# Modulation vectors on one Trainium2 core: four chunks collected in one PSUM bank by zero-spaced stationary columns, and read out by one copy and four transposes

## The chip, the cores and the metric

The kernel runs on one core of one Trainium2 chip. The time is the device time of one execution in microseconds (us), the median of three runs.

## The reference

Two blocks of a network follow each other on 256 tokens of width 2048, in float32. The first block has two attention layers (even and odd), each `x + (y @ w_out)` with an input projection `rms_norm(x) @ w_in`. The second block has a gated linear recurrence and a differential attention, and both are modulated by a condition:

```python
sc = jax.nn.silu(c)
scc = jax.nn.silu(c_ctx)
for i in range(DEPTH):
    shift, scale, gate = jnp.split(sc @ mod_w[i] + mod_b[i], 3, axis=-1)
    cshift, cscale, cgate = jnp.split(scc @ mod_w[i] + mod_b[i], 3, axis=-1)
    h_lat = rms_norm_2(x, norm_g[i]) * (1.0 + scale[:, None]) + shift[:, None]
    h_ctx = rms_norm_2(ctx, norm_g[i]) * (1.0 + cscale) + cshift
```

`mod_w` is 2 x 2048 x 6144. What is changed is the way the products `sc @ mod_w[i]` and `scc @ mod_w[i]` are collected and turned into columns: two rows (the two conditions) times 21 chunks of 512 outputs. (Three more chunks of the second layer are made elsewhere, in the second block, and stay as they are.)

## The kernel before, in words

**Units and the ring.** All weights come through a ring of 8 slots (`ring`, `raw(U)`), in units of 128 x 1024 float32 (512 KB): two k-tiles of 128 rows by 512 columns. The list `RING` sets the order of all units of the program; SyncE's queue loads unit U as soon as TensorE has used unit U - 8. A unit of a projection is split by ScalarE into a high part (`ring_hi`, line 1427) and by VectorE into a low part (`ring_lo`, line 1954), and TensorE multiplies high by high, low by high and high by low: 12 matmuls of 512 columns a unit in `multiply` (line 782).

**The modulation.** 168 of the first block's units are modulation units, 8 to a chunk of 512 outputs, laid in pairs between the projection units (`with_mod`). They are not split: `fill_mod` (line 855) multiplies them as plain float32. The stationary operand holds the conditions' columns, the moving one the weights. K-tile k goes to the 32 PSUM partitions that start at 32 * (k % 4), so that each of the four groups of 32 partitions of bank 3 holds a quarter of the sum over k. The matmul's stationary operand is 32 columns wide, of which two matter (the two conditions). All this happens in the first block's stretch of the program, between its heads' work.

**Reading a chunk out.** When the 8 units of chunk m are through, VectorE copies the bank to SBUF (`mod_rows`, line 2042). Later, ahead of the last projection unit that stands before chunk m + 1, TensorE runs `sum_mod` (line 866): four float32 matmuls with 128 columns of the copied rows as the stationary operand and the two columns of `row_sums` as the moving one (`SEL` holds ones at partitions 0, 32, 64, 96 for condition 0, and at the next ones for condition 1). They add the four quarters and turn the rows into columns at once, and write them into the same bank 3. VectorE then adds the bias and stores to `mod_t` (`mod_columns`, line 2050). The first matmul of chunk m + 1 waits for that (`mod_ready`). In the trace each plain float32 matmul stands as two records, with two LDWEIGHTS records; a transpose stands as one.

**VectorE's order.** `follow(units)` walks the same list: at the unit in `ROWS_BY` it copies the rows, at the unit in `SUMS_BY` it makes the columns, after the splits that are due there. A wait in it holds back everything behind it on VectorE.

Of the kernel before, what the change touches and what calls it, by code (L numbers as in the profile page):

```python
# [24 lines left out]
ALU = mybir.AluOpType  # L25
AX = mybir.AxisListType.X

P = 128
SEQ = 256
D = 2048  # L30
KT = D // P
TT = SEQ // P
# [38 lines left out]
CHUNK = 512  # L71
# [151 lines left out]
def chunk_units(stage, chunks, per=8):  # L223
# [63 lines left out]
POS = {unit: at for at, unit in enumerate(RING)}  # L287
# [80 lines left out]

ROWS_BY = {next(s for s in SPLIT_UNITS if s > POS["mod", 8 * m + 7]): m for m in range(N_MOD)}
SUMS_BY = {max(s for s in SPLIT_UNITS if s < POS["mod", 8 * m + 8]): m for m in range(N_MOD - 1)}  # L370
SUMS_BY[POS[OD_TURNS[-1].gaps[1][1]]] = N_MOD - 1
assert len(ROWS_BY) == len(SUMS_BY) == N_MOD and all(r <= s for r, s in zip(sorted(ROWS_BY), sorted(SUMS_BY)))

# [48 lines left out]
RES0 = {"ev_out": 0, "od_out": 4, "lru_out": 8, "att_out": 13}  # L422
MODS_BEFORE_MLA = sum(POS["mod", 8 * m + 7] < POS["ukv", 0] for m in range(N_MOD))
FEATURES_LAT, FEATURES_OD, FEATURES_CTX = 24, 27, 35
# [5 lines left out]
def build(nc, t, consts, out):  # L430
    ctx = ExitStack()
    with ctx:
        def sb(name, shape, dtype=F32, owner=ctx):
            return owner.enter_context(nc.sbuf_tensor(name, shape, dtype))
# [35 lines left out]

        def raw(U, n=UNIT):

            return RA[:, U % SLOTS, 0:n]
# [108 lines left out]
        s_hi, s_lo, s_lop, s_wused = map(sem, ("weights_hi", "weights_lo_by_vector", "weights_lo_by_gpsimd", "weight_units_used"))  # L582
        s_vt, s_vec, s_cond, s_cs = map(sem, ("vectors_transposed", "vectors_ready", "cond_hi", "cond_ready"))
        s_sq, s_sqc, s_ms, s_rt, s_rs = map(sem, ("squares_summed", "chunk_squares_summed", "mean_square", "root_taken", "rstd_ready"))
# [178 lines left out]
        def _(pe):  # L763
# [82 lines left out]
            def fill_mod(u):  # L846

                m, j = divmod(u, 8)
                U = POS["mod", u]
# [9 lines left out]
            def sum_mod(m, bank=MB):  # L859

                pe.wait_ge(s_mods, m + 1)
                if m:
                    pe.wait_ge(s_modd, m)
                rows = MODS_EV if m < MODS_OF_EVEN else MODS_OD
# [29 lines left out]
            def head_turn(turn):  # L894
# [76 lines left out]
                if turn is MLA_TURNS[1]:  # L971
                    pe.wait_ge(s_ge, evicted("ukv", 3))
                    pe.wait_ge(s_mods, MODS_BEFORE_MLA)
                    y_transposes_of("ev", 4)
                    y_transposes_of("ev", 5)
# [109 lines left out]
            def od_out(u):  # L1085
                c, j = divmod(u, 9)
                hold = None
                if u == 0:
                    hold = {1: (s_ge, evicted("od_c", 0))}
                elif j == 0:  # L1090
                    hold = {m: (s_re, RES0["od_out"] + c - 1) for m in range(TT)} if c >= 2 else {0: (s_ye, len(YT)), 1: (s_modd, N_MOD)}
                multiply(POS["od_out", u], 2 * j, 2, 18, CHUNK, [(m, 2 * (c % 2) + m) for m in range(TT)], xt, hold=hold)
# [223 lines left out]
            def gate_sums(i):  # L1316

                pe.wait_ge(s_gm, i * 16 + 16)
                for k in range(4):
                    mm = pe.matmul(PS[:, 7, 2 * P + k:2 * P + k + 1], GACC[:, k * P:(k + 1) * P], SEL[:, 2:3], start=True, stop=True)  # L1320
                mm.then_inc(s_gsum, 1)
# [620 lines left out]
        def _(dve):  # L1942
            steps = [0]

            def link(ins):

                steps[0] += 1
                ins.then_inc(s_dve, 1)
                dve.wait_ge(s_dve, steps[0])
# [89 lines left out]

            def mod_rows(m):  # L2040
                dve.wait_ge(s_wused, POS["mod", 8 * m + 7] + 1)
                dve.tensor_copy(MODS_EV if m < MODS_OF_EVEN else MODS_OD, PS[:, 3, :]).then_inc(s_mods, 1)

            def mod_columns(m, bank=3):

                dve.wait_ge(s_modt, m + 1)
                layer, c = MOD_CHUNK[m]
# [121 lines left out]
            dve.wait_ge(s_const, 16)  # L2169
            dve.tensor_reduce(SEL[:, 0:2], ident.rearrange("p (g w) -> p w g", g=4)[:, 0:2, :], AX, ALU.add)  # L2170
            dve.memset(SEL[:, 2:3], 1.0)
            for u in range(5):
# [116 lines left out]

            dve.wait_ge(s_modd, N_MOD)  # L2290
            for l in range(2):
# [528 lines left out]
```

## Time and profile before

| | |
|---|---|
| median of three runs (2495.31 to 2495.77) | 2495.64 us |
| span of the profiled execution | 2493.0 us |
| TensorE matmul busy | 2472.9 us, 99% of the span |
| VectorE busy | 1478.2 us, 59% |
| ScalarE busy | 1179.3 us, 47% |
| TensorE's granted clock | 1.000 of full speed, the whole span |

For the profiled execution only the span is given, from its first to its last instruction; the median of the runs is 2.6 us above it. PE is TensorE's matmuls and PEld its weight loads, DVE is VectorE, ACT ScalarE, SPq SyncE's queue. Matmuls are pipelined: a record lasts longer than the step from one start to the next, so costs on TensorE are read from starts, not from durations.

### The profile page before, as it was taken

To read this page: it belongs to the slowest core of one execution; us is meant where nothing else is said; L and a number is where in the kernel's file an instruction comes from. 1 tells how busy PE (TensorE), PEld (TensorE's weight loads), DVE (VectorE), ACT (ScalarE), POOL (GpSimd) and SP (SyncE) were. 2 spreads that over 40 slices of the span, in tenths; PEclk is the share of its full clock that TensorE was granted. 3 is DMA by queue.
4 is the path that set the end of the run, shared out by engine and by line. 5 is a ranking of instruction groups with operands and counts; after the bars stand their busy time and mean duration, and the time that the engine had idled before them with its cause. 6 is when DMAs were issued, how large, how long until landed. Compare 5 with 4: busy or idle time off the path is not lost.

```text
span 2493.0 us, 31492 instructions
## 1 busy us (share of the span) xinstructions
PE 2472.9 (99%) x11984; PEld 1941.0 (78%) x11984; DVE 1478.2 (59%) x1951; ACT 1179.3 (47%) x1742; POOL 265.2 (11%) x140
## 2 busy tenths in 40 slices
PE   8999999999999999999999999999999999999999
PEld 7887777777777777788777777788887887877877
DVE  6644445554545554566767677734746476665775
ACT  6644444653444444456565555624525334243463
POOL 0000000000000000002555555100300000000000
PEclk9999999999999999999999999999999999999999
DMA  7567777637787777764333332324434344344334
GB/s 278 172 216 260 249 258 247 234 103 242 231 279 243 253 261 246 251 225 149 102 95 95 89 96 88 118 93 136 136 108 152 127 127 151 111 151 128 129 106 152
DMA packets 278403, 429.43 MB, mean 172 GB/s; under 512 B 14582, under 2 KB 93196, under 8 KB 277644
## 3 DMA queue, kind: packets, MB, share of 16 engines
q1 hardware_dynamic: 277532, 422.54, 52.1%
q10 hardware_dynamic: 752, 5.26, 0.5%
q8 instruction: 80, 1.31, 0.2%
q14 instruction: 39, 0.32, 0.0%
HBM read 425.64 MB, written 2.10 MB: 172 GB/s over the span
## 4 chain that ended last, share of the span: by engine, by line
PE 96%; ACT 1%; DVE 1%; DMA 1%; issue 0%; POOL 0%; SPq 0%; DVEq 0%; ACTq 0%
PE ps L782 67%; PE ps L1174 13%; PE ps L855 3%; PE ps L1157 2%; PE ps L964 1%; PE ps L1285 1%; PE ps L937 1%; PE ps L1303 1%; PE ps L833 1%; PE ps L1129 1%; PE ps L866 1%; PE ps L949 1%; DMA ring<-in_att_w_in 0%; PE ps L1294 0%; PE ps L1192 0%
## 5 line engine op out<-in xcount | busy, mean ns | idle before, releaser
L1427 ACT CAST ring_hi<-ring 128x1024 fp32r<-128x1024 f32 (+2 forms) x598 | 619.9, 1039 | 953.9 <-PE ps L782 533.2
L1954 DVE TENSOR_TENSOR ring_lo<-ring,ring_hi 128x1024 fp32r<-128x1024 f32 (+2 forms) x520 | 626.8, 1210 | 633.6 <-ACT ring_hi L1427 631.3
L782 PE MATMUL ps<-ring_hi,act_hi 128*128 128x512 f32 (+2 forms) x1272 | 512.8, 403 | 0.7 <-ACT proj L1506 0.6
L782 PE MATMUL ps<-ring_hi,act_lo 128*128 128x512 f32 (+2 forms) x1272 | 491.7, 387 | 0.0
L782 PE MATMUL ps<-ring_lo,act_hi 128*128 128x512 f32 (+2 forms) x1272 | 490.3, 385 | 0.0
L782 PE MATMUL ps<-ring_hi,features_hi 128*128 128x512 f32 x1152 | 457.6, 397 | 1.1 <-ACT second_block L1744 0.9
L782 PE MATMUL ps<-ring_hi,features_lo 128*128 128x512 f32 x1152 | 449.2, 390 | 0.0
L782 PE MATMUL ps<-ring_lo,features_hi 128*128 128x512 f32 x1152 | 448.7, 389 | 0.0
L782 PEld LDWEIGHTS ps<-ring_hi,act_hi 128*128 128x128 f32 x1272 | 239.4, 188 | 102.1 <-issue 41.4
L782 PEld LDWEIGHTS ps<-ring_hi,act_lo 128*128 128x128 f32 x1272 | 239.2, 188 | 50.8
L782 PEld LDWEIGHTS ps<-ring_lo,act_hi 128*128 128x128 f32 x1272 | 240.0, 189 | 41.9
L782 PEld LDWEIGHTS ps<-ring_hi,features_hi 128*128 128x128 f32 x1152 | 216.4, 188 | 63.8 <-issue 20.3
L782 PEld LDWEIGHTS ps<-ring_hi,features_lo 128*128 128x128 f32 x1152 | 216.2, 188 | 45.9
L782 PEld LDWEIGHTS ps<-ring_lo,features_hi 128*128 128x128 f32 x1152 | 216.6, 188 | 42.3
L2748 POOL TENSOR_TENSOR ring_lo<-ring,ring_hi 128x1024 fp32r<-128x1024 f32 x78 | 210.0, 2700 | 338.7 <-ACT ring_hi L1427 338.6
L1174 PE MATMUL ps<-features_hi,ring_hi 128*128 128x512 f32 x480 | 192.8, 402 | 0.0
L1174 PE MATMUL ps<-features_lo,ring_hi 128*128 128x512 f32 x480 | 186.8, 389 | 0.0
L1174 PE MATMUL ps<-features_hi,ring_lo 128*128 128x512 f32 x480 | 186.8, 389 | 0.0
L1174 PEld LDWEIGHTS ps<-features_lo,ring_hi 128*128 128x128 f32 x480 | 90.1, 188 | 21.8 <-issue 3.6
L1174 PEld LDWEIGHTS ps<-features_hi,ring_hi 128*128 128x128 f32 x480 | 90.1, 188 | 21.8 <-issue 3.6
L1174 PEld LDWEIGHTS ps<-features_hi,ring_lo 128*128 128x128 f32 x480 | 90.1, 188 | 18.7
L855 PE MATMUL ps<-ring,cond_t 128*32 128x512 f32 x672 | 89.5, 605 | 0.0
(277 smaller groups left out, 2453.4 us busy)
## 6 DMA issues: line engine op xcount, KB each, us to landing
ring<-in_mod_w SPq DMA_DIRECT2D x192, 512.0 KB, 5.2
ring<-in_att_w_in SPq DMA_DIRECT2D x128, 512.0 KB, 3.7
ring<-in_ev_w_in SPq DMA_DIRECT2D x104, 512.0 KB, 4.8
ring<-in_od_w_in SPq DMA_DIRECT2D x96, 512.0 KB, 4.6
ring<-in_lru_w_in SPq DMA_DIRECT2D x64, 512.0 KB, 4.0
ring<-in_ev_w_out SPq DMA_DIRECT2D x40, 512.0 KB, 4.5
ring<-in_lru_w_out SPq DMA_DIRECT2D x40, 512.0 KB, 3.7
ring<-in_od_w_out SPq DMA_DIRECT2D x36, 512.0 KB, 4.9
```

What stands on the lines that cost most here:

```text
L782: mm = pe.matmul(PS[:, bank, 0:n], a, w[:, k - k0, :], start=(k == k_first and j == 0), stop=(k == k_last and j == 2))
L833: mm = pe.transpose(PS[:, 4 + q % 4, col:col + P], rows(tt, 2 * j + k), ident)
L855: mm = pe.matmul(PS[g:g + 32, MB, :], CS[:, 2 * k:2 * k + 32], raw(U)[:, k % 2 * CHUNK:(k % 2 + 1) * CHUNK], start=(k < 4), stop=(k >= KT ...
L866: mm = pe.matmul(PS[:, bank, 2 * j:2 * j + 2], rows[:, j * P:(j + 1) * P], SEL[:, 0:2], start=True, stop=True)
L937: mm = pe.matmul(to, qt[:, tt * P:(tt + 1) * P], kt_[:, 0:n], start=True, stop=h is not MLA)
L949: mm = pe.transpose(PS[:, 4 + a, h.p_at(kt, tt):h.p_at(kt, tt) + P], S[:, a, s:s + P], ident)
L964: mm = pe.matmul(PS[:, 6 + a, tt * P:tt * P + w], PT[:, a, h.p_at(kt, tt):h.p_at(kt, tt) + P], rows, start=(kt == 0), stop=(kt == kts[-1]))
L1157: mm = pe.matmul(PS[:, 4 + j, :], GW[:, b, j, :], XC[:, b, :, :].rearrange("p c s -> p (c s)"), start=True, stop=True)
L1174: mm = pe.matmul(PS[:, part * 2 + b, :], W[:, w], x[:, kk, :], start=(kk == 0 and j == 0), stop=(kk == KT - 1 and j == 2))
L1427: act.copy(high(U, n), raw(U, n)).then_inc(s_hi, 1)
L1954: dve.tensor_tensor(out=low(U, n), in0=raw(U, n), in1=high(U, n).bitcast(F32), op=ALU.subtract).then_inc(s_lo, 1)
L2748: pool.tensor_tensor(out=low(U), in0=raw(U), in1=high(U).bitcast(F32), op=ALU.subtract).then_inc(s_lop, 1)
```

## The change

Four chunks now form a round (the last round has one chunk: 21 chunks make 6 rounds). The conditions' columns are stored with zeros between them in `CZ`, part of the tile `scalars`: k-tile k's two columns stand at 8 * (k + 1) - 2. A window of 8 columns that starts 2 * slot earlier holds them at places 2 * slot and 2 * slot + 1, with zeros in the other six. So chunk `slot` of a round adds its two rows at its own partitions of each group and adds zeros to the others', and the stationary operand is 8 columns wide where it was 32. The bank is copied, transposed (four transposes of 128 x 128 in place of four matmuls with two columns) and reduced once a round. The sum over the four groups is now made by VectorE, one `tensor_reduce` for each condition, and the bias is added to 16 x 2 columns at once. The order of the chunks over the ring's modulation units is changed so that a round lies in one layer; which ring positions are modulation units is not.

```diff
-MODS_OF_EVEN = 12
-MOD_CHUNK = [(0, m) for m in range(10)] + [(1, 11)] + [(1, m) for m in range(8)] + [(0, 10), (0, 11)]
+MOD_CHUNK = [(0, m) for m in range(12)] + [(1, m) for m in range(8)] + [(1, 11)]
+MOD_SLOTS = 4
+MOD_COLS = 2 * MOD_SLOTS
+N_ROUND = -(-N_MOD // MOD_SLOTS)
+ROUNDS_OF_EVEN = 3
+def round_chunks(r):
+
+    return range(r * MOD_SLOTS, min((r + 1) * MOD_SLOTS, N_MOD))
+def round_end(r):
+
+    return 8 * round_chunks(r)[-1] + 7
...
+ROWS_BY = {next(s for s in SPLIT_UNITS if s > POS["mod", round_end(r)]): r for r in range(N_ROUND)}
+SUMS_BY = {max(s for s in SPLIT_UNITS if s < POS["mod", round_end(r) + 1]): r for r in range(N_ROUND - 1)}
...
-        SEL = sb("row_sums", [P, 3])
+        SEL = sb("row_sums", [P, 1])
+        CZ = SC[:, 0:(KT + 1) * MOD_COLS - 2]
...
-                if j == 0 and m:
-                    pe.wait_ge(s_modd, m)
+                if slot == 0 and j == 0 and r:
+                    pe.wait_ge(s_modd, r)
                 pe.wait_ge(s_w[U % SLOTS], landed(U))
                 for k in range(2 * j, 2 * j + 2):
-                    g = 32 * (k % 4)
-                    mm = pe.matmul(PS[g:g + 32, MB, :], CS[:, 2 * k:2 * k + 32], raw(U)[:, k % 2 * CHUNK:(k % 2 + 1) * CHUNK],
-                                   start=(k < 4), stop=(k >= KT - 4))
+                    g, first = 32 * (k % 4), (k + 1) * MOD_COLS - 2 - 2 * slot
+                    mm = pe.matmul(PS[g:g + MOD_COLS, MB, :], CZ[:, first:first + MOD_COLS], raw(U)[:, k % 2 * CHUNK:(k % 2 + 1) * CHUNK],
+                                   start=(slot == 0 and k < 4), stop=(m == round_chunks(r)[-1] and k >= KT - 4))
...
+                rows = MODS_EV if r < ROUNDS_OF_EVEN else MODS_OD
                 for j in range(4):
-                    mm = pe.matmul(PS[:, bank, 2 * j:2 * j + 2], rows[:, j * P:(j + 1) * P], SEL[:, 0:2], start=True, stop=True)
+                    mm = pe.transpose(PS[:, bank, j * P:(j + 1) * P], rows[:, j * P:(j + 1) * P], ident)
                 mm.then_inc(s_modt, 1)
...
-            pe.wait_ge(s_cs, 1)
+            pe.wait_ge(s_cz, 1)
...
+            def mod_columns(r, bank=3):
+
+                dve.wait_ge(s_modt, r + 1)
+                n = len(round_chunks(r))
+                layer, c = MOD_CHUNK[round_chunks(r)[0]]
                 first = VEC_AT["mod_b_2"] + 48 * layer + 4 * c
-                sums = PS[:, bank, 0:8].rearrange("p (k w) -> p k w", w=2)
-                dve.tensor_tensor(out=MODT[:, layer, 4 * c:4 * c + 4, :], in0=sums, in1=GT[:, first:first + 4].unsqueeze(2).to_broadcast([P, 4, 2]),
+                cols = MODT[:, layer, 4 * c:4 * c + 4 * n, :]
+                parts = PS[:, bank, :].rearrange("p (b g q) -> p b g q", b=4, g=4)
+                for w in range(2):
+                    ins = dve.tensor_reduce(cols[:, :, w].rearrange("p (s b) -> p s b", b=4),
+                                            parts[:, :, :, w:2 * n:2].rearrange("p b g s -> p s b g"), AX, ALU.add)
+                link(ins)
+                dve.tensor_tensor(out=cols, in0=cols, in1=GT[:, first:first + 4 * n].unsqueeze(2).to_broadcast([P, 4 * n, 2]),
                                   op=ALU.add).then_inc(s_modd, 1)
...
             dve.sem_inc(s_ltab, 1)
+            link(dve.memset(CZ, 0.0))
+            dve.wait_ge(s_cs, 1)
+            dve.tensor_copy(CZ[:, MOD_COLS - 2:].rearrange("p (k q) -> p k q", q=MOD_COLS)[:, :, 0:2],
+                            CS[:, 0:2 * KT].rearrange("p (k v) -> p k v", v=2)).then_inc(s_cz, 1)
```

On TensorE, behind the first chunk (`proj` is where the copied rows lie, `ring_hi`, `ring_lo` and `act_hi`, `act_lo` are the split weights and activations of a projection), before:

```order
L782 MATMUL ps<-ring_hi,act_lo 128x512
L866 MATMUL ps<-row_sums,proj 128x2 [waits mod_rows_ready]
L866 MATMUL ps<-row_sums,proj 128x2 x3
L782 MATMUL ps<-ring_hi,act_hi 128x512 [waits weights_lo_by_vector]
L782 MATMUL ps<-ring_lo,act_hi 128x512
```

The same place now:

```order
L796 MATMUL ps<-ring_hi,act_hi 128x512
L796 MATMUL ps<-ring_lo,act_hi 128x512
L796 MATMUL ps<-ring_hi,act_lo 128x512
L796 MATMUL ps<-ring_hi,act_hi 128x512 [waits weights_lo_by_vector]
L796 MATMUL ps<-ring_lo,act_hi 128x512
```

The two rows of `row_sums` are gone there, and the projection goes on without a break; this happens behind 15 of the 21 chunks.

On TensorE, behind the fourth chunk, which ends the first round, before (the last row is the next modulation unit's first matmul):

```order
L866 MATMUL ps<-row_sums,proj 128x2 [waits mod_ready,mod_rows_ready]
L866 MATMUL ps<-row_sums,proj 128x2 x3
L782 MATMUL ps<-ring_hi,act_hi 128x512 [waits weights_lo_by_vector]
...
L782 MATMUL ps<-ring_hi,act_lo 128x512
L855 MATMUL ps<-ring,cond_t 32x512 [waits weights_landed2,mod_ready]
L855 MATMUL ps<-ring,cond_t 32x512
```

The same place now:

```order
L879 MATMUL ps<-consts,proj 128x128 [waits mod_rows_ready]
L879 MATMUL ps<-consts,proj 128x128 x3
L796 MATMUL ps<-ring_hi,act_hi 128x512 [waits weights_lo_by_vector]
...
L796 MATMUL ps<-ring_hi,act_lo 128x512
L870 MATMUL ps<-ring,scalars 8x512 [waits weights_landed2,mod_ready]
L870 MATMUL ps<-ring,scalars 8x512
```

Four transposes stand where the four matmuls stood, one projection unit (12 matmuls) ahead of the next modulation unit, as before, and that unit still waits for `mod_ready`.

On VectorE at the same end of a round, before:

```order
L1954 TENSOR_TENSOR ring_lo<-ring,ring_hi 128x1024 [waits weights_hi]
L2042 COPY proj<-ps 128x512 [waits weight_units_used]
L1954 TENSOR_TENSOR ring_lo<-ring,ring_hi 128x1024 [waits weights_hi] x2
L2050 TENSOR_TENSOR mod_t<-ps,vectors_t 128x8 [waits mod_summed]
L1954 TENSOR_TENSOR ring_lo<-ring,ring_hi 128x1024 [waits weights_hi]
```

And now:

```order
L1967 TENSOR_TENSOR ring_lo<-ring,ring_hi 128x1024 [waits weights_hi]
L2055 COPY proj<-ps 128x512 [waits weight_units_used]
L1967 TENSOR_TENSOR ring_lo<-ring,ring_hi 128x1024 [waits weights_hi] x2
L2066 TENSOR_REDUCE mod_t<-ps 128x16 [waits mod_summed]
L2066 TENSOR_REDUCE mod_t<-ps 128x16
L2069 TENSOR_TENSOR mod_t<-mod_t,vectors_t 128x32 [waits vector_step]
L1967 TENSOR_TENSOR ring_lo<-ring,ring_hi 128x1024 [waits weights_hi]
```

Three linked instructions stand where one stood, still behind the two splits.

## Rows read from the trace of the kernel before

**Rows 1.** The page: span, and busy time of each engine
```profile
span 2493.0 us, 31492 instructions
PE 2472.9 (99%) x11984; PEld 1941.0 (78%) x11984; DVE 1478.2 (59%) x1951; ACT 1179.3 (47%) x1742; POOL 265.2 (11%) x140
```

**Rows 2.** Windows: length, busy of PE, PEld, DVE, ACT, POOL, PEclk, DMA share, GB/s
```profile
170.00:1060.00 890.00, 887.79 (x4622) 662.08 (x4621) 456.46 (x741) 397.48 (x611) 1.99 (x4) 1.00 0.72 240
```

**Rows 3.** The page: the chain that ended last, by engine
```profile
PE 96%; ACT 1%; DVE 1%; DMA 1%; issue 0%; POOL 0%; SPq 0%; DVEq 0%; ACTq 0%
```

**Rows 4.** Line 855, the modulation units' matmuls: duration ns min/median/max, first and last start
```profile
L855 PEld LDWEIGHTS ps<-ring,cond_t x672: 105/108/110, 175.2 to 1047.8; 128*32 128x32 f32 x168
L855 PE MATMUL ps<-ring,cond_t x672: 592/604/618, 175.2 to 1048.2; 128*32 128x512 f32 x168
```

**Rows 5.** Line 866, the sums of the first twelve chunks
```profile
L866 PEld LDWEIGHTS ps<-row_sums,proj x96: 187/192/192, 200.7 to 755.5; 128*128 128x128 f32 x96
L866 PE MATMUL ps<-row_sums,proj x96: 165/251/251, 200.9 to 755.6; 128*128 128x2 f32 x96
```

**Rows 6.** Timeline of PE around one pair of modulation units: start us, us
```profile
174.88 0.39 PE L782 MATMUL ps<-ring_hi,act_lo 128*128 128x512 f32 x1
175.20 1.07 PE L855 MATMUL ps<-ring,cond_t 128*32 128x512 f32 x8
176.20 0.50 PE L782 MATMUL ps<-ring_hi,act_hi 128*128 128x512 f32 x1
176.53 0.39 PE L782 MATMUL ps<-ring_lo,act_hi 128*128 128x512 f32 x1
176.76 0.39 PE L782 MATMUL ps<-ring_hi,act_lo 128*128 128x512 f32 x1
```

**Rows 7.** Timeline of PE around one sum
```profile
200.70 0.39 PE L782 MATMUL ps<-ring_hi,act_lo 128*128 128x512 f32 x1
200.93 0.95 PE L866 MATMUL ps<-row_sums,proj 128*128 128x2 f32 x8
201.74 0.49 PE L782 MATMUL ps<-ring_hi,act_hi 128*128 128x512 f32 x1
202.06 0.40 PE L782 MATMUL ps<-ring_lo,act_hi 128*128 128x512 f32 x1
```

**Rows 8.** Timeline of PE around four transposes
```profile
65.84 0.39 PE L782 MATMUL ps<-ring_hi,mem_lo 128*128 128x512 f32 x1
66.07 0.60 PE L833 MATMUL ps<-consts,x_res 128*128 128x128 f32 x4
...
66.73 0.39 PE L782 MATMUL ps<-ring_lo,mem_hi 128*128 128x512 f32 x1
```

**Rows 9.** Timeline at the end of the fourth chunk's sum (the window cuts off L855)
```profile
320.77 0.16 DVE L2050 TENSOR_TENSOR mod_t<-ps,vectors_t 128x8 f32<-128x8 f32 x1
321.33 0.64 PE L855 MATMUL ps<-ring,cond_t 128*32 128x512 f32 x4
```

**Rows 10.** Timeline at the end of the twelfth chunk's sum
```profile
758.33 0.39 PE L782 MATMUL ps<-ring_hi,act_lo 128*128 128x512 f32 x1
758.45 0.16 DVE L2050 TENSOR_TENSOR mod_t<-ps,vectors_t 128x8 f32<-128x8 f32 x1
758.66 0.64 PE L855 MATMUL ps<-ring,cond_t 128*32 128x512 f32 x4
```

**Rows 11.** Timeline at the end of the twentieth chunk's sum
```profile
1033.83 0.17 DVE L2050 TENSOR_TENSOR mod_t<-ps,vectors_t 128x8 f32<-128x8 f32 x1 [3.30 <-PE ps L866]
1035.26 0.64 PE L855 MATMUL ps<-ring,cond_t 128*32 128x512 f32 x4
```

**Rows 12.** Groups of DVE: busy us, mean ns of one, idle before
```profile
L1984 DVE TENSOR_REDUCE stats<-scalars 128x2 f32<-128x8 f32 x2 | 0.3, 162 | 3.1 <-ACT second_block L1460 3.1
L2195 DVE TENSOR_REDUCE scalars<-arena 128x2 f32<-128x128 f32 x1 | 0.3, 286 | 0.0
```

**Rows 13.** Waits of ACT between 170 and 1060 us, for the weights to land
```profile
ACT ring_hi L1427 <- DMA ring<-in_od_w_in: 145.0, 69, 6.7
```

More of the change, by code:

```diff
@@ L367 @@
 LAST_OF = {multiplied(*chunk) - 1: chunk for chunk in EVICTED}
[L369 to L372, printed above, removed]
+ROWS_BY = {next(s for s in SPLIT_UNITS if s > POS["mod", round_end(r)]): r for r in range(N_ROUND)}
+SUMS_BY = {max(s for s in SPLIT_UNITS if s < POS["mod", round_end(r) + 1]): r for r in range(N_ROUND - 1)}
+SUMS_BY[POS[OD_TURNS[-1].gaps[1][1]]] = N_ROUND - 1
+assert len(ROWS_BY) == len(SUMS_BY) == N_ROUND and all(r <= s for r, s in zip(sorted(ROWS_BY), sorted(SUMS_BY)))
 def evicted(stage, c):
@@ L422 @@
 RES0 = {"ev_out": 0, "od_out": 4, "lru_out": 8, "att_out": 13}
-MODS_BEFORE_MLA = sum(POS["mod", 8 * m + 7] < POS["ukv", 0] for m in range(N_MOD))
+ROUNDS_BEFORE_MLA = sum(POS["mod", round_end(r)] < POS["ukv", 0] for r in range(N_ROUND))
 FEATURES_LAT, FEATURES_OD, FEATURES_CTX = 24, 27, 35
@@ L848, in fill_mod, with sum_mod @@
                 m, j = divmod(u, 8)
+                r, slot = divmod(m, MOD_SLOTS)
                 U = POS["mod", u]
-                if j == 0 and m:
-                    pe.wait_ge(s_modd, m)
+                if slot == 0 and j == 0 and r:
+                    pe.wait_ge(s_modd, r)
                 pe.wait_ge(s_w[U % SLOTS], landed(U))
                 for k in range(2 * j, 2 * j + 2):
-                    g = 32 * (k % 4)
-                    mm = pe.matmul(PS[g:g + 32, MB, :], CS[:, 2 * k:2 * k + 32], raw(U)[:, k % 2 * CHUNK:(k % 2 + 1) * CHUNK],
-                                   start=(k < 4), stop=(k >= KT - 4))
+                    g, first = 32 * (k % 4), (k + 1) * MOD_COLS - 2 - 2 * slot
+                    mm = pe.matmul(PS[g:g + MOD_COLS, MB, :], CZ[:, first:first + MOD_COLS], raw(U)[:, k % 2 * CHUNK:(k % 2 + 1) * CHUNK],
+                                   start=(slot == 0 and k < 4), stop=(m == round_chunks(r)[-1] and k >= KT - 4))
                 mm.then_inc(s_wused, 1)
[L859 to L864, printed above, removed]
+            def sum_mod(r, bank=MB):
+                pe.wait_ge(s_mods, r + 1)
+                rows = MODS_EV if r < ROUNDS_OF_EVEN else MODS_OD
                 for j in range(4):
-                    mm = pe.matmul(PS[:, bank, 2 * j:2 * j + 2], rows[:, j * P:(j + 1) * P], SEL[:, 0:2], start=True, stop=True)
+                    mm = pe.transpose(PS[:, bank, j * P:(j + 1) * P], rows[:, j * P:(j + 1) * P], ident)
                 mm.then_inc(s_modt, 1)
@@ L972, in head_turn @@
                     pe.wait_ge(s_ge, evicted("ukv", 3))
-                    pe.wait_ge(s_mods, MODS_BEFORE_MLA)
+                    pe.wait_ge(s_mods, ROUNDS_BEFORE_MLA)
                     y_transposes_of("ev", 4)
@@ L1090, in od_out @@
                 elif j == 0:
-                    hold = {m: (s_re, RES0["od_out"] + c - 1) for m in range(TT)} if c >= 2 else {0: (s_ye, len(YT)), 1: (s_modd, N_MOD)}
+                    hold = {m: (s_re, RES0["od_out"] + c - 1) for m in range(TT)} if c >= 2 else {0: (s_ye, len(YT)), 1: (s_modd, N_ROUND)}
                 multiply(POS["od_out", u], 2 * j, 2, 18, CHUNK, [(m, 2 * (c % 2) + m) for m in range(TT)], xt, hold=hold)
@@ L1319, in gate_sums @@
                 for k in range(4):
-                    mm = pe.matmul(PS[:, 7, 2 * P + k:2 * P + k + 1], GACC[:, k * P:(k + 1) * P], SEL[:, 2:3], start=True, stop=True)
+                    mm = pe.matmul(PS[:, 7, 2 * P + k:2 * P + k + 1], GACC[:, k * P:(k + 1) * P], SEL[:, 0:1], start=True, stop=True)
                 mm.then_inc(s_gsum, 1)
@@ L2038, in residual_add, with mod_rows @@
                 ins.then_inc(s_re, 1)
[L2040 to L2047, printed above, removed]
-                first = VEC_AT["mod_b_2"] + 48 * layer + 4 * c
-                sums = PS[:, bank, 0:8].rearrange("p (k w) -> p k w", w=2)
-                dve.tensor_tensor(out=MODT[:, layer, 4 * c:4 * c + 4, :], in0=sums, in1=GT[:, first:first + 4].unsqueeze(2).to_broadcast([P, 4, 2]),
+            def mod_rows(r):
+                dve.wait_ge(s_wused, POS["mod", round_end(r)] + 1)
+                dve.tensor_copy(MODS_EV if r < ROUNDS_OF_EVEN else MODS_OD, PS[:, 3, :]).then_inc(s_mods, 1)
+            def mod_columns(r, bank=3):
+                dve.wait_ge(s_modt, r + 1)
+                n = len(round_chunks(r))
+                layer, c = MOD_CHUNK[round_chunks(r)[0]]
+                first = VEC_AT["mod_b_2"] + 48 * layer + 4 * c
+                cols = MODT[:, layer, 4 * c:4 * c + 4 * n, :]
[5 more added lines that the diff above has]
+                dve.tensor_tensor(out=cols, in0=cols, in1=GT[:, first:first + 4 * n].unsqueeze(2).to_broadcast([P, 4 * n, 2]),
                                   op=ALU.add).then_inc(s_modd, 1)
@@ L2169, in _ @@
             dve.wait_ge(s_const, 16)
-            dve.tensor_reduce(SEL[:, 0:2], ident.rearrange("p (g w) -> p w g", g=4)[:, 0:2, :], AX, ALU.add)
-            dve.memset(SEL[:, 2:3], 1.0)
+            dve.memset(SEL[:], 1.0)
             for u in range(5):
@@ L2288, in _ @@
             follow([("od_out", u) for u in range(3, 6)])
-            dve.wait_ge(s_modd, N_MOD)
+            dve.wait_ge(s_modd, N_ROUND)
             for l in range(2):
```

2 lines of the change are left out of this document (1 added, 1 removed).

## The prediction

> **What bounds the kernel now.** I read the page first. TensorE's matmuls are busy for 2472.9 of 2493.0 us and the granted clock is full throughout [rows 1, 2], and the chain that ended last runs through TensorE for 96% [rows 3]. In the stretch that holds all modulation work, 170 to 1060 us, TensorE is busy for 887.79 of 890 us, while VectorE and ScalarE are at about half and the DMA engines at 0.72 [rows 2]. So the reader is to see that whatever is taken off TensorE's queue there comes off the time, as long as the others can follow, and that work taken off VectorE is worth nothing by itself.
>
> Next I read the two lines that the change touches. Line 855 has 672 records of which each lasts 604 ns, in 84 pairs of units with eight records each [rows 4]. Line 866 has 96 records in the first twelve of the 21 sums, eight in each [rows 5]. Records overlap, so I took the cost of each group from the starts around it. The yardstick is the step of product matmuls, 176.53 to 176.76, 0.23 us [rows 6]. From the last product matmul ahead of a group to the second one behind it would be two such steps, 0.46 us, if the group were not there; I take the second one, since the first behind a group starts its successor late as well.
>
> - A pair of modulation units: 174.88 to 176.53 is 1.65 us, so it costs 1.19 us [rows 6], and 84 of them 100 us.
> - A sum: 200.70 to 202.06 is 1.36 us, so it costs 0.90 us [rows 7], and 21 of them 18.9 us.
> - Four transposes in the same surroundings: 65.84 to 66.73 is 0.89 us, so they cost 0.43 us [rows 8].
>
> The sum is dear for what it does because it loads 128 columns of stationary data eight times (192 ns a record, rows 5) to move two columns through; the transposes have four records.
>
> **The change, part by part.**
>
> *The sums go.* 21 x 0.90 = 18.9 us less on TensorE. Nothing hides this time today: the products stand in the same queue.
>
> *The transposes come.* Six rounds of four: 6 x 0.43 = 2.6 us more. The Trainium skill speaks for a higher price here ("TensorE: Matmul & The Clock Gate", Part 4, PE-mode transpose): it gives about 275 ns for a transpose within a kernel; an estimate with that figure is 24 x 0.275 = 6.6 us, and the sum would be 4 us worse. The rows have the same shape and type in the same kind of stream, four in 0.43 us, and I go by them.
>
> *The stationary operand shrinks from 32 to 8 columns.* The number of matmuls, the moving columns (512) and the groups of PSUM partitions they go to stay. What can change is the load of the stationary operand. No row has 8 columns. The nearest rows are 108 ns at 32 columns [rows 4] and 192 ns at 128 columns [rows 5], both float32 matmuls in two records: 84 ns for 96 columns, so 24 columns fewer are 21 ns a load. How many loads lie on the path? At least none: 84 x 0 = 0. At most all eight of a pair: 84 x 8 x 0.021 = 14.1 us. Eight records of 604 ns pass in 1.00 us (175.20 to 176.20, rows 6), so four run side by side and their loads too; the first load of a pair must lie open, since nothing runs in front of it. I take one: 84 x 0.021 = 1.8 us less.
>
> *VectorE's copies and adds.* 15 copies and 15 adds go and 12 reductions come. VectorE is about half idle in this stretch [rows 2], so that is zero. The cover is its idle time. If it were gone, TensorE would wait for low parts of weights.
>
> *The end of a round.* Here the change can make a new wait. TensorE runs one projection unit behind the transposes and then needs `mod_ready`. Before, VectorE's part was one add of 0.16 us. Now it is two reductions, a link and an add over 32 elements. The reductions read 64 elements; the nearest rows are 162 ns for 8 elements and 286 ns for 128 [rows 12], so about 0.22 us. Two of them and a last step like today's add, less what two neighbours on VectorE overlap, make about 0.60 us, 0.44 us more than today. Moreover TensorE arrives there earlier by 0.90 - 0.43 = 0.47 us, while VectorE at this place hangs behind splits that wait for weights to land or for the heads' softmax, not for the sum. So `mod_ready` comes up to 0.91 us later as seen from TensorE. Against that stand the margins of today, from the end of the add to the start of the next modulation pair: 321.33 - 320.93 = 0.40 us at the first round's end [rows 9], 758.66 - 758.61 = 0.05 us at the third's [rows 10], 1035.26 - 1034.00 = 1.26 us at the fifth's [rows 11]. At 0.05 us there is no stall yet, since the pair starts 0.33 us after the last product matmul [rows 10], as elsewhere (0.32, rows 6), but nothing to spare either; so 0.35 us can be spared at the first and 1.21 us at the fifth. That gives a wait of 0.91 - 0.35 = 0.56 us at the first, 0.91 us at the third and none at the fifth. The second's and the fourth's margins are larger than the fifth's. Sum 1.5 us more. The lower end is 0.5 us (VectorE moves along with TensorE), the upper end 2.5 us (reductions as dear as 0.4 us each). Behind the waiting matmul stand all later products, so such a wait is paid in full. VectorE itself only waits for the transposes, which come sooner than the sums did.
>
> *The last round* has one chunk and is read out where it was read out before. The wait for `mod_ready` behind it stands at the second output chunk of the odd layer, nine units later, and costs nothing.
>
> *The zeros.* One memset and one copy on VectorE, at about 107 us, before TensorE's first modulation pair at 175.2 us [rows 4]: some 0.4 us in VectorE's idle time, so zero. If it came late, TensorE's first pair would wait, once.
>
> The sum, against the median: 2495.64 - 18.9 + 2.6 - 1.8 + 1.5 = 2479.0 us. The durations come from one execution with a span of 2493.0 us, 2.6 us below the median; that rest lies outside the first and last instruction and I leave it as it is. In its terms the span should be 2476.4 us.
>
> **The rivals.**
>
> *All loads of a pair lie on the path.* The gain is 12.3 us more: 2466.7 us. Against it stands that eight records pass in 1.00 us. The Trainium skill ("TensorE: Matmul & The Clock Gate", LDWEIGHTS) counts a load by its columns, columns / 1.2 in ns; by that rule 24 columns are worth 20 ns, and the trace's 21 ns agrees. Chance 0.05.
>
> *The weights cannot follow.* ScalarE waits for landings for 145.0 us on the odd layer's weights alone, 69 times [rows 13]; the splits come as late as the data. If TensorE gets ahead in this stretch, it may find the low parts missing and give part of the gain back. Against it: the DMA engines are at 0.72 and TensorE loses only 2.2 us of 890 today [rows 2], and the demand rises by 16/890, less than 2%. Given back in half, the time is 2487 us (chance 0.07); given back in full, 2495.5 us (chance 0.05).
>
> *The narrow matmuls do not run side by side: slower.* If a stationary operand of 8 columns were not treated as one group of the array, as that of 32 is, a pair would take eight steps one after another. A start-to-start step of a record cannot be less than its 0.23 us (a product matmul of the same 512 columns), so 1.8 us in place of 1.00; with two passes a record, 0.46 us, it is 3.7 us. 84 pairs make +67 to +227 us: 2546 to 2706 us. It turns the sign from 16.6 / 84 = 0.2 us a pair on. For it speaks only that no row has so narrow an operand; against it, that the output still starts at partitions 0, 32, 64 and 96. Chance 0.03.
>
> **How the numbers follow.** The forecast (2479 us, own range 2475 to 2483) has a chance of 0.80, and the rivals 0.05, 0.07, 0.05 and 0.03. The range is 2472 to 2486 us: it takes the forecast with its bounds and half of each neighbouring case, and leaves out less than 2 in 10. 0.2% is 5 us, about what a measurement can tell from no change here. Faster by more than that are the forecast, the open loads and the half given back: 0.92, of which I take 0.01 off for a mishap in between. Within 0.2%: 0.05. Slower: 0.04.
>
> **What would show it.** In the profile after, line 866's eight records a chunk are gone, and 24 records of transposes stand for them; the starts around a pair of modulation units are 1.63 us apart where they were 1.65; PE's busy time falls by some 18 us and its idle time rises by about 1.5 us, at the ends of the first and third round, with the reductions' add named as what ended it. VectorE's reductions should last about 0.22 us. The granted clock stays 1.00. The prediction is wrong if TensorE shows new waits for `ring_lo` in this stretch, if the eight records of a pair take more than 1.0 us, or if the transposes of a round take more than 0.43 us.

## The result, and the profile after

The changed kernel takes 2478.64 us (median of 4 runs, 2477.48 to 2479.91) against 2495.47 us of the kernel before on the same chip (4 runs, 2494.67 to 2495.77). The ratio is 0.9933, with a 95% interval of 0.9921 to 0.9945: 16.8 us or 0.67% faster, where 16.6 us were forecast. The profiled execution took 2478.72 us, of which its span is 2476.9.

The page of the changed kernel, its head, answers to [rows 1]:

```profile
span 2476.9 us, 31153 instructions
## 1 busy us (share of the span) xinstructions
PE 2455.2 (99%) x11840; PEld 1921.5 (78%) x11840; DVE 1469.1 (59%) x1934; ACT 1179.1 (48%) x1742; POOL 265.2 (11%) x140
```

TensorE has 144 matmul records fewer (168 of the sums gone, 24 transposes new) and 17.7 us less busy time; it is still the engine that sets the time. VectorE lost 9.1 us, which by itself buys nothing.

The modulation matmuls (line 870, which was 855) of the changed kernel, duration ns min/median/max, against [rows 4]:

```profile
L870 PEld LDWEIGHTS ps<-ring,scalars x672: 85/88/90, 175.2 to 1030.4; 128*8 128x8 f32 x168
L870 PE MATMUL ps<-ring,scalars x672: 592/594/597, 175.2 to 1030.9; 128*8 128x512 f32 x168
```

Around the first pair, the timeline of TensorE against [rows 6] (start us, us):

```profile
174.88 0.39 PE L796 MATMUL ps<-ring_hi,act_lo 128*128 128x512 f32 x1
175.20 1.04 PE L870 MATMUL ps<-ring,scalars 128*8 128x512 f32 x8
176.17 0.50 PE L796 MATMUL ps<-ring_hi,act_hi 128*128 128x512 f32 x1
176.51 0.39 PE L796 MATMUL ps<-ring_lo,act_hi 128*128 128x512 f32 x1
```

A load is 20 ns shorter (88 for 108), and so is the whole pair: 174.88 to 176.51 is 1.63 us where it was 1.65. Eight loads became shorter, and the pair gained the time of one. The four groups of PSUM partitions still work side by side: eight records of 0.59 us each pass in 0.97 us (175.20 to 176.17).

Around the first round's transposes, against [rows 7] and [rows 8]:

```profile
314.15 0.39 PE L796 MATMUL ps<-ring_hi,act_lo 128*128 128x512 f32 x1
314.38 0.60 PE L879 MATMUL ps<-consts,proj 128*128 128x128 f32 x4
314.74 0.47 PE L796 MATMUL ps<-ring_hi,act_hi 128*128 128x512 f32 x1
315.05 0.39 PE L796 MATMUL ps<-ring_lo,act_hi 128*128 128x512 f32 x1
```

From 314.15 to 315.05 is 0.90 us, less two steps of 0.23: 0.44 us for a group of four, as in [rows 8].

What TensorE waited for between 170 and 1060 us in the changed kernel (us in total, times, longest):

```profile
PE ps L870 <- DVE mod_t L2069: 0.8, 1, 0.8
PE ps L922 <- ACT proj L1519: 0.8, 1, 0.8
PE ps L796 <- ACT proj L1519: 0.6, 1, 0.6
PE ps L922 <- DVE arena L2265: 0.5, 1, 0.5
PE ps L977 <- DVE arena L2150: 0.2, 1, 0.2
```

Two of the five are new. The second, third and fourth stand in the kernel before too, with the same 0.8, 0.6 and 0.5 us. The first is new; it lies at the third round's end, against [rows 10]:

```profile
748.11 0.21 DVE L2066 TENSOR_REDUCE mod_t<-ps 128x16 f32<-128x64 f32 x1
...
748.36 0.19 DVE L2069 TENSOR_TENSOR mod_t<-mod_t,vectors_t 128x32 f32<-128x32 f32 x1
748.60 0.12 PEld L870 LDWEIGHTS ps<-ring,scalars 128*8 128x8 f32 x8 [1.25 <-DVE mod_t L2069]
748.60 1.04 PE L870 MATMUL ps<-ring,scalars 128*8 128x512 f32 x8 [0.83 <-DVE mod_t L2069]
```

The last is new as well. It lies behind the last round's read-out, where VectorE's reductions and add stand ahead of two copies to `arena` that TensorE's line 977 needs:

```profile
1040.80 0.25 DVE L2066 TENSOR_REDUCE mod_t<-ps 128x4 f32<-128x16 f32 x2
1041.08 0.17 DVE L2069 TENSOR_TENSOR mod_t<-mod_t,vectors_t 128x8 f32<-128x8 f32 x1
1041.17 1.28 DVE L2150 COPY arena<-ps 128x512 f32<-128x512 f32 x2
1041.10 0.60 PE L893 MATMUL ps<-consts,proj 128*128 128x128 f32 x4
1041.90 1.83 PE L977 MATMUL ps<-mem_kv,arena 128*128 128x128 f32 x14 [0.21 <-DVE arena L2150]
```

The same place before:

```profile
1058.16 0.16 DVE L2050 TENSOR_TENSOR mod_t<-ps,vectors_t 128x8 f32<-128x8 f32 x1
1058.23 1.28 DVE L2131 COPY arena<-ps 128x512 f32<-128x512 f32 x2
1058.91 0.60 PE L880 MATMUL ps<-consts,proj 128*128 128x128 f32 x4
1059.35 1.39 PE L964 MATMUL ps<-mem_kv,arena 128*128 128x128 f32 x11
```

From the four transposes (line 893, before 880) to the matmul that needs the copies it is 0.80 us, where it was 0.44. With the 0.1 us by which the matmul behind it starts late as well, the place costs 0.5 us.

**A yardstick for all runs.** All kernels here run the same other instructions on TensorE. So I took the starts of the same two of them, a product matmul at about 135 us and a transpose at about 1065 us, on either side of all modulation work, and compared the stretch between. It leaves out what differs from execution to execution at the start and behind. Each stretch is that of one execution, and its landings of weights differ: two executions of the changed kernel agree within 0.06 us, but one place, told below, moved by up to 0.5 us.

| kernel | stretch, us | against before | median, us | median of the kernel before, beside it |
|---|---|---|---|---|
| before | 930.20 | | 2495.47 | |
| changed | 912.84 | -17.36 | 2478.64 | 2495.47 |
| changed, again | 912.90 | -17.30 | 2478.11 | 2494.95 |
| narrow only | 928.52 | -1.68 | 2492.88 | 2494.95 |
| rounds of one chunk | 920.14 | -10.06 | 2487.90 | 2494.95 |
| third round earlier | 912.24 | -17.96 | 2477.08 | 2494.95 |
| sums twice | 948.78 | +18.58 | 2520.98 | 2495.39 |
| half more sums | 941.17 | +10.97 | 2504.26 | 2495.01 |
| transposes twice | 914.63 | -15.57 | 2479.94 | 2495.39 |
| fours | 913.17 | -17.03 | 2479.16 | 2495.39 |
| fours and earlier | 911.38 | -18.82 | 2479.25 | 2495.39 |
| late fours | 910.42 | -19.78 | 2475.57 | 2495.01 |

### The profile page after: what moved, and what is told of

Read it like the earlier page. It is cut to its first block, busy times and chain, and to the rows that moved or that the text cites. A ratio compares the mean times of both kernels' runs of the same rounds, so it can differ in the third digit from the quotient of the medians.

```text
span 2476.9 us, 31153 instructions
## 1 busy us (share of the span) xinstructions
PE 2455.2 (99%) x11840; PEld 1921.5 (78%) x11840; DVE 1469.1 (59%) x1934; ACT 1179.1 (48%) x1742; POOL 265.2 (11%) x140
## 4 chain that ended last, share of the span: by engine, by line
PE 96%; DVE 1%; ACT 1%; DMA 1%; issue 1%; POOL 0%; SPq 0%; DVEq 0%; ACTq 0%
PE ps L796 67%; PE ps L1187 13%; PE ps L870 3%; PE ps L1170 2%; PE ps L977 1%; PE ps L1298 1%; PE ps L950 1%; PE ps L1316 1%; PE ps L847 1%; PE ps L1142 1%; PE ps L962 1%; DMA ring<-in_att_w_in 1%; PE ps L1307 0%; PE ps L1205 0%; ACT ring_hi L1440 0%
## 5 line engine op out<-in xcount | busy, mean ns | idle before, releaser
L1187 PEld LDWEIGHTS ps<-features_hi,ring_lo 128*128 128x128 f32 x480 | 90.1, 188 | 18.7
L870 PE MATMUL ps<-ring,scalars 128*8 128x512 f32 x672 | 87.8, 594 | 0.8 <-DVE mod_t L2069 0.8
```

What stands on the lines that cost most here:

```text
L870: mm = pe.matmul(PS[g:g + MOD_COLS, MB, :], CZ[:, first:first + MOD_COLS], raw(U)[:, k % 2 * CHUNK:(k % 2 + 1) * CHUNK], start=(slot == 0 ...
L1187: mm = pe.matmul(PS[:, part * 2 + b, :], W[:, w], x[:, kk, :], start=(kk == 0 and j == 0), stop=(kk == KT - 1 and j == 2))
```

## The experiments

The theory is that of the prediction: the time is TensorE's own, 0.9 us a sum and 0.43 us a group of transposes, one open load a pair, and a wait where a round's end has no time to spare. The rivals: all loads of a pair lie on the path; or what counts is how seldom VectorE copies and waits; or the stretch behind, not the change, accounts for part of it.

**The changed kernel again**, unedited.

> The changed kernel once more, unedited, to tell what belongs to it from what belongs to one execution. Theory: the first block again ends some 17.3 us earlier than in the kernel before, and the 1.3 us that the profiled execution gave back between 1900 and 2250 us, far behind the change, come out at another size, between 0 and 3 us; median 2478.6 within 1.5 us. Rival, that the give-back is caused by the shifted work: it has the same size and stands at the same places again.

Median 2478.11 us, ratio 0.9933 (0.9919 to 0.9946). The stretch is the same within 0.06 us. Behind it, the two changed executions differ: 1424.01 us from the transpose at 1048 us to the last matmul in the first, 1422.97 in this one, 1422.65 in the kernel before. So 1.0 of the 1.3 us that the first profile lost there belong to that execution, and the change's own gain in the stretch is 17.3 us. Not all of it reaches the time: the medians are 16.8 us apart in both measurements, so about 0.5 us are given back outside the stretch. The other kernels with transposes lose between 0.4 and 2.5 us behind it in their profiles, narrow only and half more sums 0.1 us; why is not shown.

**Narrow only.**

```diff
-                    mm = pe.matmul(PS[g:g + 32, MB, :], CS[:, 2 * k:2 * k + 32], raw(U)[:, k % 2 * CHUNK:(k % 2 + 1) * CHUNK],
+                    mm = pe.matmul(PS[g:g + 8, MB, :], CS[:, 2 * k:2 * k + 8], raw(U)[:, k % 2 * CHUNK:(k % 2 + 1) * CHUNK],
```

> The kernel before, with the stationary operand cut from 32 to 8 columns and nothing else; the 6 columns beside the two conditions are those of the next k-tiles, and the sums leave their rows out. Theory of one open load a pair: 84 x 0.02 = 1.7 us less, about 2493.8 us. Rival of all eight loads on the path: 14 us less, about 2481.5 us. Rival that the width costs nothing: 2495.5 us.

Median 2492.88 us, ratio 0.9992 (0.9983 to 1.0001). The medians are 2.1 us apart, which the interval does not tell from nothing; the stretch, 1.68 us shorter, does: it is 84 x 0.020. All eight loads on the path would have been 14 us. The part that is left, 17.36 - 1.68 = 15.7 us, comes from the read-out.

**Rounds of one chunk.**

```diff
-MOD_SLOTS = 4
+MOD_SLOTS = 1
-ROUNDS_OF_EVEN = 3
+ROUNDS_OF_EVEN = 12
```

> The changed kernel with rounds of one chunk: 21 copies, 21 groups of four transposes, 42 reductions, and 2 columns of stationary data. It changes the kind of read-out without making it rarer. Theory, by TensorE's time alone: 15 more groups of transposes at 0.43 us are 6.5 us more than the changed kernel, 6 columns fewer are 0.4 us less, and the ends of chunks that have no time to spare (the third, fourth and sixth round's places and others like them, 0.05 to 0.7 us of margin today) wait for the longer chain, 1 to 4 us: 2486 to 2489 us. Rival, that what counts is how seldom VectorE copies and waits: the gain is gone with the rarity, 2495 us.

Median 2487.90 us, ratio 0.9971 (0.9961 to 0.9982). VectorE copies as often as before, waits for TensorE as often and has more to do, and the kernel is 7 us faster: rarity is not what counts for VectorE. TensorE's terms give the stretch: 21 x (0.44 - 0.90) = -9.7, and the pair, with 2 columns, is 26 ns shorter than with 32 (gap of 1288 ns for 1314), -2.2. The waits of TensorE show what was given back:

```profile
PE ps L870 <- DVE mod_t L2069: 1.6, 3, 0.7
```

That view counts only the time in which no matmul ran. By the gaps around the five pairs that start late it is 2.1 us, and the wait behind the last read-out, the same as in the changed kernel, is another 0.5: -9.7 - 2.2 + 2.1 + 0.5 = -9.3, where -10.06 was measured. The other 0.8 us lie in many steps of under 0.1 us each, and I can't name their cause. The median gained only 7.05 us: 3.0 us are lost outside the stretch, 2.5 of them behind it in the profile (last section). So the median fell into the expected 2486 to 2489 us with the help of a loss that the expectation didn't have. Of the 16.3 us that the read-out gains with rounds of four, 9.7 thus come from the kind of operation, and 6.6 from having six groups of transposes on TensorE and not 21. The kind gains because four transposes are four records and four float32 matmuls are eight: the starts of both are 0.11 us apart, whether 128 columns move or two.

**Sums twice, and half more.** The kernel before with `for j in (0, 1, 2, 3) * 2`, and in a second kernel `for j in (0, 1, 0, 1, 2, 3)`, around the sum's matmuls.

```diff
-                for j in range(4):
+                for j in (0, 1, 2, 3) * 2:
                     mm = pe.matmul(PS[:, bank, 2 * j:2 * j + 2], rows[:, j * P:(j + 1) * P], SEL[:, 0:2], start=True, stop=True)
```

> The kernel before with each chunk's four sum matmuls run twice in a row, the second time over the same result. Theory, that a sum's price is TensorE's own time: eight more records of 0.1 us each and no new turn of the stream, so 21 x 0.86 = 18 us more, about 2513 us. Rival, that the sums were cheap and the gain came from VectorE's copies and waits: nearly nothing more, 2495 to 2498 us. Some of it may be a little higher, where the add already came just in time (0.05 us of margin at four places): up to 3 us more.

> The kernel before with two of each chunk's four sum matmuls run twice. Theory: 21 x 4 records at 0.11 us are 9.2 us more by the end of the first block. The run with all four twice lost a further 8 us between 2050 and 2280 us, in an attention loop that the edit does not touch, with a wait ended by issue and a lower clock behind it. If that comes from where TensorE's longer program stands, this one, half as much longer, shows it smaller or not at all: 2504.6 us without it, up to 2513 us with it.

Sums twice: 2520.98 us, ratio 1.0104 (1.0089 to 1.0119). Half more: 2504.26 us, ratio 1.0039 (1.0025 to 1.0053). TensorE around a doubled sum:

```profile
199.78 0.39 PE L782 MATMUL ps<-ring_hi,act_lo 128*128 128x512 f32 x1
200.00 1.84 PE L866 MATMUL ps<-row_sums,proj 128*128 128x2 f32 x16
201.71 0.49 PE L782 MATMUL ps<-ring_hi,act_hi 128*128 128x512 f32 x1
```

From 199.78 to 201.71 is 1.93 us; in [rows 7] the same distance is 1.04. The second set costs 0.89 us, and 21 of them 18.7; the stretch grew by 18.58. So a sum's price is TensorE's time, 0.11 us a record, and nothing hides it; the rival of 2495 to 2498 us is out. Half more adds 0.447 us to each sum, 9.4 us in all, and its median is 9.3 us above the kernel before; its profiled execution lost another 1.6 us in the stretch (below). The median of sums twice, though, is 25.6 us up: 7 us more than the stretch explains. Those stand elsewhere, and are told in the last section.

**Transposes twice.** The changed kernel with `for j in (0, 1, 2, 3) * 2:` around `pe.transpose`.

> The changed kernel with each round's four transposes run twice. Theory: 24 more transposes at 0.109 us are 2.6 us more, plus up to 0.4 us of later read-out at the first and third round's ends: 2480.7 to 2482 us. With 0.275 us a transpose it would be 6.6 us more, 2485 us.

Median 2479.94 us, ratio 0.9940 (0.9925 to 0.9955). The stretch is 1.79 us longer than in the changed kernel, where 2.6 were expected. Each doubled group costs 0.437 us on TensorE (1022 ns for 585 from one product matmul to the next), 2.6 us for six; but at the third round's end it fills 0.41 us of the wait that stood there (a gap of 1787 ns around the pair in place of 2193). That leaves 2.2. And the wait behind the last read-out is gone: from the transposes to the matmul that needs the copies it is 0.44 us again (0.80 in the changed kernel), 0.5 us less with the step behind it. So 2.6 - 0.4 - 0.5 = 1.7, and 1.79 was measured. TensorE comes later at both places, and VectorE's work there is done in time. The median lies 0.8 us below the expected range for the same reason. At 0.275 us a transpose, the price of the prediction's estimate, it would have been 6.6.

**The third round read out earlier.**

```diff
-SUMS_BY = {max(s for s in SPLIT_UNITS if s < POS["mod", round_end(r) + 1]): r for r in range(N_ROUND - 1)}
+SUMS_BY = {sorted(s for s in SPLIT_UNITS if s < POS["mod", round_end(r) + 1])[-2 if r == 2 else -1]: r for r in range(N_ROUND - 1)}
```

> The changed kernel with the third round's transposes and reductions one projection unit earlier, where the copy had been done for 8.7 us. Theory: the wait of 0.9 us on TensorE ahead of the next modulation pair (the gap of 2193 ns where others have 1294) goes, nothing takes its place, and the time is 0.9 us less, which is within the noise of the median but shows in the trace. Rival: the wait only moves, since the margin was given by the splits and not by the reductions; the first block ends at the same time.

Median 2477.08 us, ratio 0.9929 (0.9916 to 0.9943). The timeline at the third round's end shows the wait gone:

```profile
746.99 0.19 DVE L2069 TENSOR_TENSOR mod_t<-mod_t,vectors_t 128x32 f32<-128x32 f32 x1
748.43 0.12 PEld L870 LDWEIGHTS ps<-ring,scalars 128*8 128x8 f32 x8 [0.35 <-issue]
```

The add ends 1.25 us ahead of the pair, in place of 0.05, and the 0.35 us ended by issue are the turn of the stream that every pair has. The stretch gained 0.60 us and not 0.90, because in this execution the first round's end waited 0.3 us (a gap of 1610 ns around the pair for 1294). That place hangs on when two units of weights land: its margin from the add to the pair was 0.36, 0.55 and 0.06 us in the three executions so far of kernels that are alike up to there.

**Fours.** Two neighbouring pairs in one gap are laid together, twelve times, where no round ends between them; then the same with the earlier third round; then only the seven behind 500 us.

```diff
     if pairs == 2 and n in (3, 4):
         places = [1, 3]
+    done = PAIRS_LAID[0]
+    places = [places[j - 1] if j % 2 and (done + j) % 16 else places[j] for j in range(pairs)]
+    PAIRS_LAID[0] += pairs
```

(`late_fours` adds `and done + j > 21` to the condition, and has the earlier third round too.)

> The changed kernel with twelve times two neighbouring pairs of modulation units laid together as fours (two pairs in the same gap at the same place), where no round ends between them. Theory: a pair costs 1.17 us, of which 0.87 us are the two passes of four matmuls side by side, and 0.3 us the turn of the stream to narrow operands and back; twelve turns fewer are 3.5 us less, 2475 us. Rival: four unsplit units in a row empty the ring of eight slots faster than the weights land, and TensorE waits for the next weights or for low parts: the gain is lost or turned round, 2478 to 2485 us, with new waits for landings or for ring_lo on TensorE.

> Both together: the fours, and the third round's transposes one projection unit earlier. Theory: 3.5 + 0.9 us less than the changed kernel, 2474 us, with no gap over 1.7 us around a modulation group of two units. Rival: the margins at the ends of the rounds move with the fours, and another round's end waits instead; then it equals the fours alone.

> The changed kernel with the third round read out one projection unit earlier, and fours only at the seven places behind 500 us, where the profile of the twelve fours shows a plain gap of 2.15 us; the five ahead of that, four of which waited for low parts, are pairs again. Theory: 7 x 0.31 = 2.2 us less than with the earlier read-out alone, 2475 us, and the first block ends 18.5 + 1.3 = 19.8 us earlier than in the kernel before. Rival: a four that stood without a wait did so because TensorE had lost time before it; then new waits for low parts come up at these places and the end stays where it was.

Fours: 2479.16 us, ratio 0.9935 (0.9922 to 0.9949), no gain. A four by itself is worth what was expected: from the product matmul ahead of it to the second one behind it, less two steps, it costs 2.03 us, where two pairs cost 2 x 1.17. But TensorE waits at four of the twelve, between 170 and 400 us:

```profile
PE ps L800 <- DVE ring_lo L1971: 3.9, 4, 1.5
```

One of them, with its 16 records, and the wait behind them:

```profile
262.25 1.90 PE L874 MATMUL ps<-ring,scalars 128*8 128x512 f32 x16
265.45 0.19 PEld L800 LDWEIGHTS ps<-ring_hi,act_hi 128*128 128x128 f32 x1 [2.23 <-DVE ring_lo L1971]
265.45 0.50 PE L800 MATMUL ps<-ring_hi,act_hi 128*128 128x512 f32 x1 [1.30 <-DVE ring_lo L1971]
```

The 3.9 us eat the 3.7 us of twelve turns. The rival named low parts that come late because the weights land late. ScalarE's casts ahead of these low parts bear that out at the first of the four places, where TensorE waits 1.5 us, and not at the one shown:

```profile
185.93 1.04 ACT L1444 CAST ring_hi<-ring 128x1024 fp32r<-128x1024 f32 x1 [9.20 <-DMA ring<-in_ev_w_in]
262.53 2.92 ACT L1444 CAST ring_hi<-ring 128x1024 fp32r<-128x1024 f32 x3
```

At 185.93 us ScalarE had waited for a landing. At 262.53, as at the two other places (212.63 and 361.13 us), it had been busy with the head's softmax until then and waited for nothing; at 262 us VectorE had other work as well until 264.0. So the rival's sign came, its cause is shown at one place, and at three the low parts come late behind the heads' work. With the earlier third round the stretch is 1.8 us shorter (-18.82 for -17.03), half of it because the waits for `ring_lo` are 2.9 us in that execution and not 3.9. The median, 2479.25 us, ratio 0.9937 (0.9923 to 0.9950), does not show it. Two of its five executions (2480.2 and 2480.4 us), and one of the five of the fours (2480.1), are those with a mean granted clock of 0.999 and not 1.000; what lowered it there is not shown.

Late fours: 2475.57 us, ratio 0.9922 (0.9908 to 0.9935), with no wait for `ring_lo` left and the lowest median of all. Against the third round earlier alone (2477.08) it is 1.5 us, and the stretch 1.82 us shorter; 7 x 0.31 = 2.2 were expected; two of the seven fours have gaps that are 0.2 and 0.1 us longer than the others', and the first round's end waited 0.5 us where the run compared with had 0.3. Against the changed kernel it is 0.12%, within what the intervals leave open. But the stretch is 2.42 us shorter, and all five executions (2474.5 to 2475.9 us) lie below all nine of the changed kernel (2477.1 to 2479.9).

## Why the prediction was right

The large terms, the sums that go and the transposes that come, were right in mechanism and size, and experiments show both. The small term for the ends of the rounds came out near its size by luck.

- **The sums go: 18.9 us.** Held. Doubling them costs 18.58 us in the stretch, and the places of the sums are 16.4 us shorter together, where 18.9 - 2.6 = 16.3 were forecast.
- **The transposes come: 2.6 us.** Held: 0.44 us a group after, 0.437 us for a doubled one. The prediction called itself wrong at more than 0.43 us; the 0.01 us over it is the rounding of the timeline. The Trainium skill's figure of about 275 ns a transpose ("TensorE: Matmul & The Clock Gate", Part 4) does not fit a stream like this as a cost: the starts are 0.11 us apart. The record itself lasts 272 ns, which agrees with the page's figure as the duration of one, and that is not what a transpose costs among others.
- **Narrow operands: 1.8 us, one open load a pair.** Held, and shown alone: 1.68 us. The slope was taken from 128 and 32 columns, 21 ns for 24 columns; 20 came out, and 26 for 30. The rival with all eight loads on the path is out.
- **The end of a round: 1.5 us.** Right in mechanism, too large by 0.6 in sum, and a like wait of 0.5 us at a place where none was forecast (next point) nearly made up for it. At the third round's end the forecast was 0.91 us, and the gap grew by 0.90 (2193 ns for 1294). The reductions last 218 ns (0.22 forecast). At the first round's end 0.56 us were forecast and none came in this execution: I held VectorE fixed while TensorE came earlier, but its add came earlier too (317.30 us, 2.92 behind the start of the transposes; before, 3.37 behind the start of the sum). Two later kernels, alike up to there, did wait, 0.3 and 0.5 us. The margins at the second, fourth and fifth ends sufficed.
- **The last round: nothing.** Wrong by 0.5 us. `mod_ready` cost nothing there, as forecast. But VectorE's longer read-out stands ahead of its copies to `arena`, and TensorE comes there earlier: it waits for the copies. The prediction had looked only at what waits for the read-out, not at what stands behind it on VectorE. Transposes twice, in which TensorE comes 0.44 us later, lacks this wait.
- **VectorE's copies, adds and the zeros: nothing.** The work taken away is worth nothing, as forecast: rounds of one chunk keep all 21 copies and still gain 10 us in the stretch. Its idle time did not cover everything added, as the last round shows.
- **The weights cannot follow.** Not at this size: no wait for `ring_lo` or a landing on TensorE. But late low parts are the next limit: the fours met them at four places, at one of them because of a landing.
- **The sum.** -18.9 + 2.6 - 1.7 + 0.9 + 0.5 = -16.6 us by the corrected terms, -17.36 in the stretch, -16.8 between the medians. With the places added up in nanoseconds the terms give -16.9 us; the 0.5 us left in the stretch lie in many small steps that I can't assign, and about as much is given back outside it. That the median came within 0.2 us of the forecast is finer than the working behind it.

## What to carry to other kernels

Where one engine is busy for 99% of a stretch, price a group of its instructions by the starts around it: the distance between the neighbours with the group, less their usual step. That gave 0.90 us for a sum and 0.43 for four transposes, and each cost 0.89 and 0.44 us when it was run twice, where the records' own durations (0.6 us for a matmul of which four run at once, 0.25 us for one of two columns) give nonsense. A record with 128 stationary columns cost 0.11 us here, whether two columns moved or 128, so count records, and make such read-outs rare before making them narrow. (That the stationary load sets the 0.11 us is likely, but no run changed it alone.) And a read-out made rarer and longer needs its consumer's margin checked at each place where it is waited for: one of five had none, and a second ran out in two later kernels. What stands behind the read-out on the same engine needs the same look: there the last round cost 0.5 us.

## What the runs showed of the hardware

**A stall of TensorE that no semaphore explains, and the clock behind it.** Sums twice lost about 7 us more behind the change, in an attention loop that no edit touches: all four runs took 2519.4 to 2523.2 us. In its profile, 8.7 us behind, 6.3 of them lie between 2077.9 and 2089.3 us, where TensorE stands still twice, ended by issue:

```profile
2077.81 0.38 PE L1272 MATMUL ps<-consts,second_block 128*128 128x128 f32 x2
2079.38 1.13 PE L1285 MATMUL ps<-second_block 64*128 64x512 f32 x4 [1.19 <-issue]
2080.44 0.50 PE L782 MATMUL ps<-ring_hi,features_hi 128*128 128x512 f32 x1
2083.16 0.80 PE L782 MATMUL ps<-ring_lo,features_hi 128*128 128x512 f32 x1 [2.21 <-issue]
2083.75 0.63 PE L782 MATMUL ps<-ring_hi,features_lo 128*128 128x512 f32 x1
2084.18 0.63 PE L782 MATMUL ps<-ring_hi,features_hi 128*128 128x512 f32 x1
```

The windows of that stretch (length; busy of PE, PEld, DVE, ACT, POOL; PEclk; DMA share; GB/s):

```profile
2080.00:2083.00 3.00, 0.94 (x5) 0.19 (x1) 2.90 (x4) 0.57 (x2) 0.00 (x0) 0.82 0.29 109
2083.00:2087.00 4.00, 3.84 (x9) 3.07 (x10) 0.61 (x1) 0.91 (x4) 0.00 (x0) 0.50 0.02 4
```

In the first window TensorE was busy for 0.94 of the 3 us, and the granted clock fell in it (0.82 in the mean); in the second it was 0.50, its level of 1.2 GHz: the products' step is 0.43 us (2083.75 to 2084.18) where it is 0.23. Rounds of one chunk show a wait of 1.7 us ended by issue at the same place, with the clock held. Half more sums shows none there, and its median loses nothing behind the stretch. Rounds of one chunk have 84 records of read-out on TensorE, the kernel before 168, half more sums 252 and sums twice 336; the first and the last stall. So it is not just a matter of how long TensorE's program is. The loss shows in the medians of both kernels, so it belongs to the kernel and not to one execution; what it hangs on stays open.

**A lower clock without a stall of that size.** In the profiled execution of half more sums, at 1043 us:

```profile
1040.00:1043.00 3.00, 2.22 (x21) 2.08 (x20) 0.00 (x0) 2.07 (x4) 0.00 (x0) 1.00 0.61 192
1043.00:1046.00 3.00, 3.00 (x19) 2.75 (x22) 0.76 (x2) 0.20 (x1) 0.00 (x0) 0.55 0.05 20
```

TensorE had waited 0.78 us for ScalarE and then run short matmuls, busy for 2.22 of 3 us, and then ran at a granted clock of 0.55 for 3 us, which cost 1.5 of the 1.6 us above. The kernel before waits the same 0.78 us at this place, with four sum matmuls behind it in place of six, and sums twice has eight; both keep their clock there. The execution took 2506.26 us where the median is 2504.26. One more of the five, with 2506.39 us, has the same mean clock of 0.999, and the other three, with 1.000, took 2503.6 to 2504.3. Why these two and not the others is not shown.
